# Whole banks and real tokens only behind the second layer's attention, with the layer loop written out

## What is computed

```python
h = concatenate([meta, x])                          # 16 + 512 = 528 tokens
for l in range(2):                                  # the two layers of block 1
    hn = rmsnorm(h, norm1_g[l])
    q, k, v, u = split(hn @ w_in[l])
    attn = diff_attention(rope(q), rope(k), v, ...) # causal, over all 528 tokens
    conv = conformer_conv(u + b_glu[l], ...)        # 31 taps, causal
    h = h + concatenate([attn, conv]) @ w_out[l]    # "out" stage
    hn = rmsnorm(h, norm2_g[l])
    gate, up = split(hn @ w_gate_up[l])             # 1024 -> 2 x 2816
    h = h + (silu(gate) * up) @ w_down[l]           # 2816 -> 1024
h = rmsnorm(h, final_g)[:, 16:]                     # the meta tokens end here
... block 2 on h ...
```

## Time and profile before

| | us |
|---|---|
| median of 3 runs | 2745.92 (2742.92 to 2750.82) |
| span of the profiled execution | 2734.5 |
| median less span | 11.4 |
| PE busy in the span | 2590.8 (95%) |
| POOL busy | 1323.5 (48%) |
| DVE, ACT busy | 1150.0 (42%), 980.2 (36%) |

### The profile page before, as it was taken

The page is one execution under the profiler, slowest core; times in us unless marked ns, Lnnn a source line. Parts: engine busy times, 40 slices in busy tenths (PEclk is TensorE's granted clock), DMA queues, the critical chain, the costliest instruction groups (busy, mean ns, idle before and its releaser), DMA issues.

```text
span 2734.5 us, 47648 instructions
## 1 busy us (share of the span) xinstructions
PE 2590.8 (95%) x18759; PEld 2315.0 (85%) x18759; DVE 1150.0 (42%) x2015; ACT 980.2 (36%) x1744; POOL 1323.5 (48%) x790
## 2 busy tenths in 40 slices
PE   8988999999997999999899898999999989999999
PEld 7957999999994999999878688788777767788887
DVE  6874421125687432122667544202566613320210
ACT  4344422223435332222456321433555542321221
POOL 4762765568574466566744310223111155564562
PEclk9999999999998999999899899999999999999999
DMA  5210222322220122232313000312111142232322
GB/s 159 78 47 17 92 80 79 104 81 89 94 64 30 34 91 84 94 98 69 100 58 112 17 2 17 93 62 64 53 47 47 47 162 78 76 108 93 92 92 77
DMA packets 175678, 203.93 MB, mean 75 GB/s; under 512 B 6436, under 2 KB 160647, under 8 KB 175255
## 3 DMA queue, kind: packets, MB, share of 16 engines
q1 hardware_dynamic: 172176, 199.57, 22.6%
q10 hardware_dynamic: 3334, 2.06, 0.3%
HBM read 193.23 MB, written 8.39 MB: 74 GB/s over the span
## 4 chain that ended last, share of the span: by engine, by line
PE 80%; POOL 5%; issue 4%; DVE 3%; ACT 2%; POOLq 2%; DVEq 1%; DMA 1%; SPq 0%; ACTq 0%
PE ps L739 17%; PE ps L740 17%; PE ps L741 17%; PE ps L1620 7%; POOL wlo L2941 4%; PE ps L990 3%; PE ps L1489 3%; POOLq L2986 2%; PE ps L1471 1%; PE ps L1434 1%; POOL conv L2984 1%; PE ps L1213 1%; PE ps L1459 1%; PE ps L1247 1%; PE ps L1450 1%
## 5 line engine op out<-in xcount | busy, mean ns | idle before, releaser
L2941 POOL TENSOR_TENSOR wlo<-wraw,whi 128x1024 fp32r<-128x1024 f32 x364 | 875.4, 2426 | 894.3 <-ACT whi L1704 894.1
L739 PE MATMUL ps<-hn_hi,whi 128*128 128x264 f32 (+1 forms) x2752 | 889.1, 323 | 22.1 <-POOL wlo L2941 9.7
L740 PE MATMUL ps<-hn_lo,whi 128*128 128x264 f32 (+1 forms) x2752 | 876.9, 319 | 0.0
L741 PE MATMUL ps<-hn_hi,wlo 128*128 128x264 f32 (+1 forms) x2752 | 875.5, 318 | 0.0
L739 PEld LDWEIGHTS ps<-hn_hi,whi 128*128 128x128 f32 x2752 | 521.6, 190 | 60.3 <-issue 18.8
L741 PEld LDWEIGHTS ps<-hn_hi,wlo 128*128 128x128 f32 x2752 | 520.9, 189 | 35.6
L740 PEld LDWEIGHTS ps<-hn_lo,whi 128*128 128x128 f32 x2752 | 521.9, 190 | 31.6
L1704 ACT CAST whi<-wraw 128x2048 fp32r<-128x2048 f32 x182 | 346.6, 1904 | 556.1 <-PE ps L741 380.9
L739 PE MATMUL ps<-ff_hi,whi 128*128 128x264 f32 x704 | 201.0, 285 | 4.1 <-POOL wlo L2941 4.1
L741 PE MATMUL ps<-ff_hi,wlo 128*128 128x264 f32 x704 | 200.3, 285 | 0.0
L740 PE MATMUL ps<-ff_lo,whi 128*128 128x264 f32 x704 | 199.9, 284 | 0.0
(11 more groups left out here) (489 smaller groups left out, 4301.3 us busy)
## 6 DMA issues: line engine op xcount, KB each, us to landing
wraw<-in_w_in SPq DMA_DIRECT2D x54, 1024.0 KB, 5.3
wraw<-in_w_gate_up SPq DMA_DIRECT2D x44, 1024.0 KB, 5.1
wraw<-in_w_up SPq DMA_DIRECT2D x16, 1024.0 KB, 5.4
wraw<-in_w_down SPq DMA_DIRECT2D x16, 1024.0 KB, 5.0
wraw<-in_w_out SPq DMA_DIRECT2D x12, 1024.0 KB, 5.1
wraw<-in_w_down SPq DMA_DIRECT2D x16, 768.0 KB, 4.4
wraw<-in_w_down SPq DMA_DIRECT2D x16, 640.0 KB, 4.0
gate_dram<-gate_out SPq DMA_DIRECT2D x16, 256.0 KB, 2.1
```

The lines of the kernel that those rows point to most:

```text
L739: nc.tensor.matmul(dst, whi[:, slot, c:c + P], rhs_hi, start=start, stop=False)
L740: nc.tensor.matmul(dst, whi[:, slot, c:c + P], rhs_lo, start=False, stop=False)
L741: return nc.tensor.matmul(dst, wlo[:, slot, c:c + P], rhs_hi, start=False, stop=stop)
L2941: last = nc.gpsimd.tensor_tensor(wlo[:, slot, part], wraw[:, slot, part], whi[:, slot, part].bitcast(F32), ALU.subtract)
```

## The change

Only block 1 is touched. The loop over the two layers is written out on each of the five engines (`for l in range(DEPTH)` in Python), so that the second layer has code of its own and the semaphore values of `l` are constants. In the second layer (`l == DEPTH - 1`) the out stage works on tokens 16 to 527 in halves of 256, and the feed forward on the same 512 tokens in one fill of a whole bank instead of two of 264: two fills per panel instead of four, numbered `j` = 1 and 3, each of which counts for two on the semaphores. All elementwise steps between are made 512 wide in the same way. The first layer, the projections, attention, convolution, and the norm at the end (still 528 wide) stay as they are. The inner loops over pairs of panels remain loops.

```diff
+        HALVES = [(j, j // 2, HALF * (j % 2), HALF, 1) for j in range(4)]
+        WHOLES = [(2 * oc + 1, oc, N_META, SEQ, 2) for oc in range(2)]
+        def ff_parts(l):
+            return WHOLES if l == DEPTH - 1 else HALVES
+        def out_tokens(l, f):
+            n = SEQ // 2 if l == DEPTH - 1 else HALF
+            a = N_META + n * (f % 2) if l == DEPTH - 1 else n * (f % 2)
+            return slice(a, a + n), n
+        def glu_piece(x, l, j, oc, n):
+            return x.rearrange(flat)[:, oc * SEQ:(oc + 1) * SEQ] if l == DEPTH - 1 else x[:, j, :]
...
-            with pe.Fori(0, DEPTH) as l:
+            for l in range(DEPTH):
...
-                        for j in range(4):
-                            oc, half = j // 2, j % 2
+                        for j, oc, a, w, count in parts:
                             if glu_at is not None and s == 0:
                                 pe.wait_ge(glu_used, glu_at + (j + 1))
...
-                                last = product(ps[:, bank, 0:HALF], s, k, oc,
-                                               hn(hn_hi, k, HALF * half, HALF),
-                                               hn(hn_lo, k, HALF * half, HALF), k == 0, k == KD - 1)
-                            last.then_inc(products_done, 1)
+                                last = product(ps[:, bank, 0:w], s, k, oc, hn(hn_hi, k, a, w), hn(hn_lo, k, a, w),
+                                               k == 0, k == KD - 1)
+                            last.then_inc(products_done, count)
...
-                        dst = ps[:, wo_bank(f), 0:HALF]
+                        dst = ps[:, wo_bank(f), 0:w]
...
-                                for j in range(4):
-                                    oc, half = j // 2, j % 2
+                                for j, oc, a, w, count in ff_parts(l):
...
-                                        last = product(ps[:, 4 * b + j, 0:HALF], s, k, oc, ff_hi[:, kf, a:a + HALF],
-                                                       ff_lo[:, kf, a:a + HALF], kf == 0, kf == n - 1)
+                                        last = product(ps[:, 4 * b + j, 0:w], s, k, oc, ff_hi[:, kf, a:a + w],
+                                                       ff_lo[:, kf, a:a + w], kf == 0, kf == n - 1)
...
-                            nc.vector.tensor_tensor(glu_val[:, j, :], ps[:, 4 + j, 0:HALF], glu_gate[:, j, :],
-                                                    ALU.mult).then_inc(glu_used, 1)
+                            v = glu_piece(glu_val, l, j, oc, w)
+                            nc.vector.tensor_tensor(v, ps[:, 4 + j, 0:w], glu_piece(glu_gate, l, j, oc, w),
+                                                    ALU.mult).then_inc(glu_used, count)
                             dve.drain()
...
+                            nc.vector.tensor_copy(ff_hi[:, ds(i * 2 + oc, 1), a:a + w].rearrange(flat), v
+                                                  ).then_inc(ffv_hi, count)
...
-                            for j in range(4):
-                                c = 2 * b + j // 2
+                            for j, oc, a, w, count in ff_parts(l):
+                                c = 2 * b + oc
                                 dve.wait_ge(products_done, ev + (EV_DOWN[part] + 5 * b + 1 + j + 1))
-                                x = h[:, c, HALF * (j % 2):HALF * (j % 2 + 1)]
-                                nc.vector.tensor_tensor(x, x, ps[:, 4 * (b % 2) + j, 0:HALF], ALU.add).then_inc(h_added, 1)
+                                x = h[:, c, a:a + w]
+                                nc.vector.tensor_tensor(x, x, ps[:, 4 * (b % 2) + j, 0:w], ALU.add).then_inc(h_added, count)
                                 if j % 2:
                                     dve.drain()
                                     gain(l * 16 + 16, c, lambda c: lay[:, NEXT + c:NEXT + c + 1])
```

More of the change, by code:

```diff
@@ L984, in out_fill @@
                         if k0:
[L985 removed]
+                            x_hi, x_lo = (hn(x, k0 + k, own.start, w) for x in (hn_hi, hn_lo))
                         else:
[L987 to L990 removed]
+                            x_hi, x_lo = (x[:, k, own] for x in (att_hi, att_lo))
+                        dst = ps[:, wo_bank(f), 0:w]
+                        for i, (wt, x) in enumerate(((whi, x_hi), (whi, x_lo), (wlo, x_hi))):
+                            last = nc.tensor.matmul(dst, wt[:, j % 2, c:c + P], x, start=(k == 0 and i == 0),
                                                     stop=(k == 3 and i == 2))
@@ L1740, in _ @@
             act.wait_ge(table_in, 16)
-            with act.Fori(0, DEPTH) as l:
+            for l in range(DEPTH):
                 use0 = l * (PANELS_L // 2)
@@ L2956, in _ @@
             lower(1, 1)
-            with pool.Fori(0, DEPTH) as l:
+            for l in range(DEPTH):
                 first = l * PANELS_L
```

85 lines of the change are left out of this document (39 added, 46 removed).

## The result

| | before | after |
|---|---|---|
| median of four runs each, us | 2746.94 (2742.92 to 2750.82) | 2725.26 (2720.03 to 2727.56, and one of 3611.82) |
| ratio, 95% interval | | 0.9935 (0.9914 to 0.9957) |
| profiled execution: span, its own time, us | 2734.5 | 2725.8, 2727.56 |

The 2725.26 counts a slow run of 3611.82 us, whose mean granted clock was 0.65; the ratio leaves it out, and the other three runs have a median of 2722.97 us.

What follows compares the result with a forecast made beforehand. PE's matmuls were taken to bound most of layer 2's feed forward. Terms of 16.6 + 4.5 + 0 + 1.5 + 1.9 - 1.0 = 23.5 us saved gave a span of 2711.0, with 11.4 around it 2722.4; predicted 2722.5, range 2715 to 2730.

Steps and rivals of the forecast that it cites:

- Term 1: Layer 2's gate/up and down: one 512-column fill for two of 264 saves 15.7 ns per pair; 16.6 and 4.5 us counted.
- the first rival: Whole-bank matmuls in layer 2's feed forward stand 233.3 ns apart, saving 11.3 ns a pair: 2728.3 us; chance 0.16.
- The split of term 1: Of 15.7 ns saved per pair of fills, 6.7 from the 16 columns left out, 9.0 from the second instruction.
- Term 2: Layer 2's down part 1: saving of 3.8 us turns into 4 us more waits for `wlo`, 6.0 in sum; 0 gained.
- Term 3: Layer 2's out stage: 384 matmuls at 118.3 instead of 122.3 ns save 1.5 us, bounds 0.8 and 1.5.
- Term 4: Between layers 1 and 2: writing out the loop removes the jump back, 1.9 us saved, bound 0.
- edits with no cost: Constant semaphore values save register instructions: 0 gained, up to 2 us if attention's short steps feel them.
- Term 5: Longer last additions at gate/up part 1's start (0.3 us) and part 1's end (0.7): 1.0 lost, bounds 0.5 and 2.
- 11.4 around the span: Time added to the forecast span of 2711.0 us to give 2722.4, the median of the runs less 23.5.
- Part 1 keeps its saving: Rival: in down part 1 `gained` falls into POOL's gaps, up to 3.8 us more saved, 2718.7 us; chance 0.17.
- Code stalls: Rival: the longer program stalls the queues in layer 2, no faster from 12 stalls, about 2754 us from 17; chance 0.03.
- The two widths cost the same: Rival: the change gains nothing per layer, only if PE were not the bound in gate/up; no chance of its own given.

Runs made afterwards that it cites:

- halves of 256: Changed kernel, but layer 2's feed forward takes the 512 real tokens in two fills of 256 per chunk; gate/up part 0 took 136.92 us (135.30 in the changed kernel).
- order_shift: Changed kernel with chunk splits on ACT and low parts on POOL one slot later in down part 1, both layers; 2721.80 us, ratio to before 0.9927.
- unroll: Kernel before with only the layer loop written out, both layers still in halves of 264; ratios to before 0.9977 and 0.9973.
- order_hn: Changed kernel with layer 2's `hn` packed at 512, ACT's casts before splits in three blocks, POOL ordered as in order_shift; 2720.14 us, ratio to before 0.9909.

## Why the prediction was right, and where it was not

**The direction, the range and most places held.** 2725.3 us lies in 2715 to 2730, and so does 2722.97, the median of the other three runs; the kernel is faster by 0.65% in the first comparison and by 0.74% on the mean of three.

**Term 1 is the step that failed, in its size.** I took 228.9 ns from block 2 for "that loop of lines 739 to 741" and argued from the code's lines. The lines were the same, the operand's layout was not. Measured are 232.8 ns, so a pair saves 11.8 ns: 15.4 us over the three stages instead of 21.1 less the added wait. That is nearly the first rival's number (233.3 ns, 11.3 ns a pair), which I gave 0.16. The difference that I saw between the two stretches, a bank changed with each weight tile, is not the one: the loop here doesn't do that, and moving the banks changed nothing. For gate/up, 1056 of the 1344 pairs, the runs put it down to the distance of `hn`'s chunks. For `ff` (232.8 ns) the cause is open, since 512 did not mend it. The rule of the Trainium skill weighed there (TensorE: Matmul & The Clock Gate, "Back-to-back issue gap") would have given 9.2 ns a pair. The same section of the Trainium skill gives that formula for an isolated matmul; for a stream of weight loads and matmuls, as this one is, it gives about 131 ns at 512 columns, which the prediction did not weigh and which no stretch here comes near (228.9 to 233.3 ns). The measured 11.8 lies between formula and forecast, and no matmul here stands as close to the columns' time as the formula has it: 11.2 ns above it at 256 columns (117.9), 12.3 at 264, 15.6 to 20.0 at 512.

**The split of term 1** into 6.7 ns of columns and 9.0 of the second instruction fell too: 8.8 and 3.0 (halves of 256).

**Term 2 was right**: nothing gained, in the mechanism (cast behind the squares behind `gained`) and in the number of waits. Their sum was 4.65 us and not 6.0, with longer panels in its place. POOL's idle time ahead of `wlo` in the kernel after shows the cast as the cause, and order_shift, which took that queue away, brought 3.2 us back.

**Term 3**: 0.84 us measured over the last 216 matmuls (26.45 to 25.61), as its lower bound; the other 168 lie among attention steps, whose clock varies by more.

**Term 4**: 1.87 us against 1.9, shown by unroll alone. Its companion, "edits with no cost: 0, up to 2", may be too low. Two comparisons of unroll give 3 to 4 us that the ledger doesn't hold, at the edge of what they can tell; that is open.

**Term 5**: 0.16 and 0.65 us, in sum 0.8 against 1.0.

**The base.** The prediction added "11.4 around the span". In every later run the time stands only 1.7 to 2.0 us above its profiled span (2727.56 and 2725.8 here). So some 9.5 us of the 11.4 were, in all likelihood, a profiled execution of before that happened to be faster than the three timed ones. A span of 2734.5 and 1.8 around it make 2736.3, below every timed run of before (2737.22 is the lowest). The total came out by the median all the same, as the prediction had subtracted the same 23.5 from it; but the difference of two profiled spans (8.7 us here) would have misled.

**Why the time comes nearer to 2722.5 than the terms do.** The ledger's 17.5 us would have put it at 2728.4, 5.9 us above the forecast. The remainder of unroll (3 to 4 us) may fill part of that gap, the attention's clock moves single times by up to 8 us, and 2725.26 and 2722.97 are medians of few runs. That the forecast number came out so near is in part luck; the direction and the place of most of the gain are not.

**The rivals.** "Part 1 keeps its saving" fell: 61.25 us, not 58. "Code stalls" fell: the three stretches of the written-out second layer that work in whole banks have no issue waits on PE, and unroll is faster, not slower. "The two widths cost the same" fell.

## What to carry to other kernels

Read the spacing of matmuls from a stretch whose moving operand is laid out like the new one's, not only from the same line of code; between two layouts the spacing of the same instruction differed by 4 ns, a third of what this change saved per pair. Where an engine's queue holds a wait ahead of the next weights' cast, as in the down stage here, a faster TensorE may gain nothing. Moving the cast ahead gives the time back only if the end of the stage is looked at as well, since what was moved lands on the sums that the next stage waits for. And before a change of 0.7% is priced from one profile, profile the same kernel twice: layer 2's feed forward stages repeated to 0.1 us, attention only to 8 us.

## What the runs showed of the hardware that was not expected

- Where the moving operand lies in SBUF changes the spacing of 512-column matmuls: 229.1 ns at 512 columns a chunk, 233.0 at 528, for `hn`; starting at column 0 or 16 of the row makes nothing (135.31 and 135.30 us for the stage). For `ff` it is 232.3 to 232.8 ns at 528 and 233.3 at 512, and for block 2's `f_hi` 233.3 at 512, so nothing general follows.
- A jump back over a whole layer's code cost PE 1.87 us and DVE 3.14 us of issue; written out, neither is there.
- A tensor-tensor of 0.7 us on DVE took 2.84 us beside POOL's instructions, and such steps, not matmuls, decided when block 2 could start in order_shift and order_hn.
- The same program's attention in layer 1 took 142.7 us in one execution and 150.3 in another, at a mean granted clock of 0.92 and 0.88, with PE equally busy in the stretch shown (59.39 and 59.47 of 60 us).
